# Folding the last two experts' rows into the token sums on TensorE, in a 64-expert kernel on Trainium2

## The reference, cut to what matters

```python
gp = softmax(xt @ w_grp + b_grp); g_p, g_idx = top_k(gp, 1)       # one of 8 groups
e_p, e_loc = top_k(softmax(el_sel), 2); e_p = e_p / sum(e_p)      # two of its 8 experts
weights = g_p * e_p                                               # per token and choice
for each expert e, on the tokens that chose it:
    y = (silu(x @ w1[e]) * (x @ w3[e])) @ w2[e]
h = h + g2 * sum over the two choices of weight * y
out = rmsnorm(h, final_g)
```

## Time and profile before

| | us |
|---|---|
| runs | 2423.55, 2425.97, 2429.41 |
| median of the runs | 2425.97 |
| span of the profiled execution | 2425.2 |
| first expert matmul of the profiled execution | 1452.7 |
| end of the last expert matmul | 2397.4 |
| start of the last DVE operation (L2903) | 2420.84 |

### The profile page before, as it was taken

The page is one execution under the profiler, slowest core; times in us unless marked ns, Lnnn a source line. Parts: engine busy times, 40 slices in busy tenths (PEclk is TensorE's granted clock), DMA queues, the critical chain, the costliest instruction groups (busy, mean ns, idle before and its releaser), DMA issues. The chain is left out here.

```text
span 2425.2 us, 26229 instructions
## 1 busy us (share of the span) xinstructions
PE 2267.0 (93%) x10596; PEld 1416.4 (58%) x10596; DVE 1048.8 (43%) x1730; ACT 718.5 (30%) x1163; POOL 783.4 (32%) x491
## 2 busy tenths in 40 slices
PE   8999999999999999999999999888888888888887
PEld 6676578888887787777777873222222222322233
DVE  6666654443456999746765233111111111211112
ACT  5435643222233333557674221000000000000001
POOL 3335655545553443433336521111111011101000
PEclk9999999999999999999999999999999999999999
DMA  4222243534545243253345269999999999999996
GB/s 161 99 101 68 96 140 113 200 134 162 190 122 139 71 104 109 75 170 120 131 153 205 104 269 412 425 422 424 424 425 425 426 426 425 427 425 426 427 426 272
DMA packets 175417, 598.76 MB, mean 247 GB/s; under 512 B 18098, under 2 KB 96946, under 8 KB 149696
## 3 DMA queue, kind: packets, MB, share of 16 engines
q1 hardware_dynamic: 156000, 564.39, 59.8%
q10 hardware_dynamic: 8704, 24.22, 2.6%
q0 software_dynamic: 10592, 8.46, 1.1%
HBM read 593.19 MB, written 28.97 MB: 257 GB/s over the span
## 5 line engine op out<-in xcount | busy, mean ns | idle before, releaser
L2923 POOL TENSOR_TENSOR ring_r<-ring,ring_r 128x1024 fp32r<-128x1024 f32 (+2 forms) x215 | 513.3, 2393 | 650.2 <-ACT ring_r L1544 650.0
L857 PE MATMUL ps<-r,ring_r 128*128 128x512 f32 x1512 | 605.3, 400 | 3.8 <-POOL ring_r L2923 1.5
L859 PE MATMUL ps<-r,ring_r 128*128 128x512 f32 x1512 | 590.5, 391 | 0.0
L858 PE MATMUL ps<-r,ring_r 128*128 128x512 f32 x1512 | 590.1, 390 | 0.0
L1555 ACT ACTIVATE arena<-ps 128x512 f32<-128x512 f32 (+4 forms) x200 | 150.5, 761 | 1046.8 <-PE ps L1420 852.8
L1420 PE MATMUL ps<-arena 128*64 128x512 f32 x672 | 317.9, 629 | 68.7 <-DMA arena<-in_w 68.5
L1418 PE MATMUL ps<-arena 128*64 128x512 f32 x672 | 328.8, 639 | 0.9 <-DMA arena<-in_w 0.9
L1544 ACT ACTIVATE ring_r<-ring 128x1024 fp32r<-128x1024 f32 x220 | 222.8, 1015 | 351.9 <-PE ps L859 192.1
L857 PEld LDWEIGHTS ps<-r,ring_r 128*128 128x128 f32 x1512 | 282.9, 187 | 75.3 <-issue 10.5
L3028 POOL DMA_INDIRECT y_d<-arena,cbm x64 | 63.7, 995 | 805.0 <-DVE arena L2876 539.6
L858 PEld LDWEIGHTS ps<-r,ring_r 128*128 128x128 f32 x1512 | 282.9, 187 | 64.3 <-issue 5.8
(11 more groups left out here) (377 smaller groups left out, 2550.8 us busy)
## 6 DMA issues: line engine op xcount, KB each, us to landing
arena<-in_w SPq DMA_DIRECT2D x105, 2048.0 KB, 33.7
ring<-in_w SPq DMA_DIRECT2D x86, 2048.0 KB, 37.0
ring<-in_w_ada SPq DMA_DIRECT2D x12, 2048.0 KB, 7.9
ring<-in_ffn_w_in SPq DMA_DIRECT2D x22, 1024.0 KB, 7.6
ring<-in_w_in SPq DMA_DIRECT2D x40, 512.0 KB, 6.2
ring<-in_w_in SPq DMA_DIRECT2D x8, 2048.0 KB, 9.3
ring<-in_fox_w_in SPq DMA_DIRECT2D x7, 2048.0 KB, 8.4
arena<-acs_d SPq DMA_DIRECT2D x16, 512.0 KB, 3.6
```

The costliest lines, as they stand in the source:

```text
L857: e.matmul(out, wh[:, k, :], X.hi[:, k0 + k, :], start=first and k == 0, stop=False)
L858: e.matmul(out, wh[:, k, :], X.lo[:, k0 + k, :], start=False, stop=False)
L859: m = e.matmul(out, wl[:, k, :], X.hi[:, k0 + k, :], start=False, stop=last and k == nk - 1)
L2923: e.tensor_tensor(GL[t], grans[t][1], GH[t].bitcast(F32), ALU.subtract).then_inc(sem["gr_lo"], 1)
```

## The change

Experts 62 and 63 (`LATE`) no longer go through `y_d`. For each of them a matrix of 128 by 512 numbers (`GIVEN`) is made at the start of the expert stage: its row is a seat (the 64 seats stand twice, in partitions 0 to 63 and in 64 to 127), its column a token, its entry the token's weight for that expert if the token sits there, and 0 otherwise. DVE makes it token by seat (`shares`: two operations of 128x4, two of 128x4x64 and one of 128x512 for an expert), PE transposes it (four 128x128 each, use "late"), DVE copies it out of PSUM (`keep_shares`) into places of the constants and parameters that nothing reads any more. ACT's silu of expert 0 waits for `shares`, since it writes over SEAT; ACT's loads of g2 and final_g wait for the transposes.

At the end PE's `late(tt)` multiplies GIVEN with `YO` of 62 and of 63 (for each tile, expert and half one matmul of 64 rows by 128 columns, 512 wide; half 0 in rows 0 to 63, half 1 in rows 64 to 127, each half into its own bank) in the place of `kept(tt)`. The residual is now added by DVE: `second(tt)` makes y1 * weight + h2t, and `total(tt)` adds that to the sums. The rows of `y_d` are read back when the scatters of experts 60 and 61 have landed. Rows that no expert writes any more must be 0, so ACT fills `y_d` with zeros early (4 MiB, DRAM to DRAM, 2048 rows of 2 KB from one row of zeros). The read-back buffers Y and OUT move up by 4096, off the slot of w2[63]. `over_blocks` now stands between the rest of expert 61 and turn(63), and its count is read at n = 32. The last banks are numbered anew.

```diff
+LATE = (NE - 2, NE - 1)
 # bank_table
+        if n == 1:
+            for ex in LATE:
+                t("late", ex)
-            t("my", n - 2)
+            t("my", n - 2, bank=7 if n - 2 == NE - 1 else None)
-            t("sum", tt, half, bank=(4 + 2 * tt + half) % 8)
+            t("sum", tt, half, bank=2 * tt + half)
 # pe
-            for n in range(NE + 2):
+            for n in range(NE):
...
                     turn(n - 1)
+                if n == 1:
+                    for i, ex in enumerate(LATE):
+                        u = ps("late", ex)
+                        w.wait_ge(sem["wk"], 4 + i)
+                        w.wait_ge(u.free, u.n)
+                        for tt in range(4):
+                            m = e.transpose(u.ap[:, 128 * tt:128 * tt + 128], PAIRED[i][:, tt].rearrange("p h x -> p (h x)"), ident)
+                        m.then_inc(u.full, 1)
...
-            over_blocks(e, over_count(e), block)
+            over_blocks(e, over, block)
+            turn(NE - 1)
+            result(NE - 2)
+            result(NE - 1)
...
-                    e.matmul(u.ap, ident, h2t[:, tt, 512 * half:512 * half + 512], start=True, stop=False)
+            def late(tt):
+                for ex in LATE:
+                    uy = ps("my", ex)
+                    w.wait_ge(uy.free, uy.n + 1)
+                    for half in range(2):
+                        u = ps("sum", tt, half)
+                        w.wait_ge(u.free, u.n)
+                        at = slice(64 * half, 64 * half + 64)
+                        e.matmul(u.ap, GIVEN[ex][at, 128 * tt:128 * tt + 128], YO[ex % 2][at, :], start=ex == LATE[0], stop=False)
...
-            kept(0)
-            kept(1)
-            w.wait_ge(osem["end"], 1)
-            kept(2)
-            kept(3)
+            for tt in range(4):
+                late(tt)
             for tt in range(4):
                 gated(tt)
 # act
+            e.dma_start(a["y_d"], a["zeros"].broadcast_to([4 * T, D // 2])).then_inc(sem["out"], 16)
...
+                if ex == 0:
+                    w.wait_ge(sem["wk"], 5)
...
+                    u = ps("late", LATE[1])
+                    w.wait_ge(u.full, u.n + 1)
...
-            over_blocks(e, over_count(e), block)
+            over_blocks(e, over, block)
+            gate_half(NE - 1)
 # dve
+            def shares(j):
+
+                ex = LATE[j]
+                for i in range(2):
+                    e.tensor_tensor(CHOSEN[:, i], OH[i][:, :, ex:ex + 1], WK[i], ALU.mult).then_inc(d.next(), 1)
+                last()
+                for i, dst in enumerate((msel, OHS)):
+                    e.tensor_tensor(dst, SEAT[:, i], CHOSEN[:, i].broadcast_to([128, 4, 64]), ALU.mult).then_inc(d.next(), 1)
+                last()
+                both = [x.rearrange("p t (o x) -> p t o x", o=1).broadcast_to([128, 4, 2, 64]) for x in (msel, OHS)]
+                e.tensor_tensor(PAIRED[j], both[0], both[1], ALU.add).then_inc(sem["wk"], 1)
...
+            def second(tt):
+                y1 = Y[tt][1]
+                w.wait_ge(sem[f"in{tt}"], 16 + 16 + 32)
+                e.scalar_tensor_tensor(y1, y1, KEEP[:, 4 + tt:5 + tt], h2t[:, tt, :], ALU.mult, ALU.add).then_inc(d.next(), 1)
...
-                w.wait_ge(sem[f"in{tt}"], 16 + 16 + 32)
...
-                e.scalar_tensor_tensor(cols(y0, 2), cols(y1, 2), KEEP[:, 4 + tt:5 + tt], PS[:, b:b + 2, :], ALU.mult, ALU.add).then_inc(sem["fc_d"], 1)
+                last()
+                e.tensor_tensor(cols(y0, 2), cols(y1, 2), PS[:, b:b + 2, :], ALU.add).then_inc(sem["fc_d"], 1)
...
+            second(0)
             total(0)
             for tt in range(1, 4):
+                second(tt)
                 total(tt)
                 normed(tt - 1)
             normed(3)
 # sp
-            for ex in (NE - 2, NE - 1):
+            for ex in (NE - 4, NE - 3):
                 u = ps("my", ex)
                 w.wait_ge(u.free, u.n + 1)
-                w.wait_ge(sem[f"yo{ex % 2}"], 16 * NE // 2)
+                w.wait_ge(sem[f"yo{ex % 2}"], 16 * (ex // 2 + 1))
```

More of the change, by code:

```diff
@@ L686, in build_program @@
         SL = [view(10752 + 256 * i, 4, 64) for i in range(2)]
-        EW = [A[:, 12288 + WC * i:12288 + WC * (i + 1)] for i in range(3)]
+        EW = [A[:, 16384 + WC * i:16384 + WC * (i + 1)] for i in range(3)]
         OXG, OXT = XG[0][0:BLK, :], view(2048, 8, BLK)
@@ L1462, in pe @@
                     result(n - 2)
+                if n == 32:
+                    over = over_count(e)
             def block(at, done):
@@ L2028, in gate_half @@
                 e.activation(SL[ex % 2], cols(u.ap, 4)[:, :, 0:64], ACT.Silu).then_inc(sem["sl"], 1)
-            for n in range(NE + 1):
+            for n in range(NE):
+                if n == 32:
+                    over = over_count(e)
                 if n == 2:
+                    u = ps("late", LATE[1])
+                    w.wait_ge(u.full, u.n + 1)
                     for i in range(2):
@@ new lines, in keep_shares, with halved, scaled @@
+            def keep_shares(j):
+                u = ps("late", LATE[j])
+                w.wait_ge(u.full, u.n + 1)
+                e.tensor_copy(GIVEN[LATE[j]], u.ap).then_inc(u.free, 1)
+            def halved(ex):
+                u = ps("mt", ex)
+                w.wait_ge(sem["sl"], ex + 1)
+                e.tensor_tensor(HT[ex % 2], SL[ex % 2], cols(u.ap, 4)[:, :, 64:128], ALU.mult).then_inc(u.free, 1)
+            def scaled(ex):
+                u = ps("my", ex)
+                if ex >= 2:
+                    w.wait_ge(sem[f"yo{ex % 2}"], 16 * (ex // 2))
+                w.wait_ge(sem["g2b"], 32)
+                w.wait_ge(u.full, u.n + 1)
+                e.tensor_tensor(YO[ex % 2], u.ap, G2, ALU.mult).then_inc(u.free, 1)
@@ new lines, in dve @@
+            for n in range(NE):
+                if n % 2 == 0 and n + 2 < NE:
+                    rows(n // 2 + 1)
+                if n == 1:
+                    shares(0)
+                    shares(1)
+                if n >= 1:
+                    halved(n - 1)
+                if n == 1:
+                    keep_shares(0)
+                    keep_shares(1)
+                if n >= 2:
+                    scaled(n - 2)
+                if n == 32:
+                    over = over_count(e)
@@ L3047, in pool @@
             rows(1)
-            for n in range(NE + 2):
+            for n in range(NE):
                 if n % 2 == 0 and n + 4 < NE:
                     rows(n // 2 + 2)
+                if n == 2:
+                    w.wait_ge(sem["out"], 16)
+                if n == 32:
+                    over = over_count(e)
                 if n == 3:
@@ L3184, in sp @@
                 e.dma_start(a["out"][tt * 128:(tt + 1) * 128, :], OUT[tt]).then_inc(sem["out"], 16)
-            w.wait_ge(sem["out"], 64)
+            w.wait_ge(sem["out"], 80)
         block = ctx.enter_context(nc.Block())
@@ L3267, in arrays @@
         "w_mix_out": x["w_mix_out_2"][0], "w1": x["w1_2"][0], "w3": x["w3_2"][0], "w2": x["w2_2"][0],
-        "final_g": x["final_g_2"].reshape(1, D),
+        "final_g": x["final_g_2"].reshape(1, D), "zeros": np.zeros((1, D // 2), np.float32),
     }
```

43 lines of the change are left out of this document (15 added, 28 removed).

## The result

The changed kernel takes **2442.15 us** in the median (2441.13 to 2442.47); in the same comparison the kernel before takes 2427.31 (2423.55 to 2429.41). The ratio is 1.0066, with a 95% interval of 1.0054 to 1.0078: slower, by 14.8 us. The forecast was 2425.0 us, in a range of 2421.5 to 2431.5, so the time lies 10.7 us above the range. The profiled execution has a span of 2440.5 us, against 2425.2.

What follows compares the result with a forecast made beforehand. Weights filling the DMA engines set 2365 us, then 32 us of PE and 28 us of tail; the last operation 0.9 us earlier gave 2425.2 - 0.9 = 2424.3 us profiled, 2425.0 us as median; range 2421.5 to 2431.5 us.

Steps and rivals of the forecast that it cites:

- The zeros: ACT's 4 MiB DMA near 198 us: cost taken as 0; upper bound the transfer's length, 10 to 20 us, little exposed.
- The last of the prediction's signs of being wrong: Last in the list of observations that would prove the forecast wrong: the attention stage is longer; no size given.
- Rival (b): Early stage: zeros hold up ACT or a load, or 2.1 us at 1470 us leave a weight-stream hole; +2 to +6 us, chance 0.12.
- The read-back: Tail: reading y_d waits for expert 61's scatter, so is issued at 2394.4 to 2394.9 us instead of 2402.0, 7.1 us earlier.
- the quiet microsecond: 2394 to 2395 us, DMA engines moving 12 GB/s: taken to show expert 61's scatter lands no later than 2394.2 us.
- PE's late matmuls: Tail: 32 instructions on the chain, halves at once, 0.86 us a pair, from 2397.3 to 2404.3 us.
- rival (a): PE's late matmuls at the end: the halves run one after the other, 1.71 us a pair; +5.8 us, 2431.8 us, chance 0.12.
- DVE's end: Tail: DVE sets the pace, 3.91 us between later totals; last operation starts at 2419.9 us against 2420.84, 0.9 us earlier.
- The start of the expert stage: Near 1466 to 1470 us: shares take 4.0 us, expert 2 is 2.1 us late, full DMA queue covers it; cost 0.
- Where the weights end: End of the expert stage: last wait for a matrix at 2365 us, with 32 us of PE behind it.
- (c): Tail: the rows alone set the end; -7.1 us, 2418.9 us, chance 0.05.
- (d): Tail: nothing moves, as expert 61's scatter lands late or SP's issue is held up; +1.8 us, 2427.8 us, chance 0.06.

## Why the prediction was wrong, point by point

**The zeros: the step that failed.** The prediction took 0 for them, on the DMA share of 0.00 from 200 to 205 us and on ACT's wait for PE, with 10 to 20 us as the transfer's length and "little of it exposed". Each of these failed.
- *The length.* It was worked out from a rate of 200 to 400 GB/s that no row showed for this kind of copy; 40.3 us were measured (4.19 MB, 104 GB/s), two to four times the estimate. No row of the kernel before could have given it, since it has no copy from DRAM to DRAM. The `c_d` reads are no such row, though their 512 KB in 5.1 us, times eight, make 41 us. That is luck: two of them together moved 233 GB/s from 214 to 218 us, and the 5.1 us have about 1 us ahead of the first bytes and the other read's bytes in them.
- *What is due behind it.* I looked 5 us of DMA idleness ahead, and at ACT. With 40 us the question is who reads between 197 and 237 us. In the changed kernel these are four `c_d` reads, two from 213.0 and two from 227.3 us, with POOL and PE directly behind them: POOL waited 18.2 us and PE stood 15.20 us. Even with my own upper bound of 20 us the transfer would have reached to 217 us, over the first `c_d` read at 213.
- *The exposure.* In its order of work PE had nothing else at that place, so the wait came through whole, 15.20 us, and more behind it. These are PE's rows, of the kernel before and then of the changed one:

```profile
226.48 0.60 PE L1077 MATMUL ps<-consts_sb,arena 128*128 128x128 f32 x4
...
229.33 0.82 PE L1077 MATMUL ps<-consts_sb,scr 128*128 128x128 f32 x6
```
```profile
241.82 1.12 PE L1087 MATMUL ps<-consts_sb,arena 128*128 128x128 f32 x4 [15.20 <-POOL arena L3044]
...
244.87 0.63 PE L1055 MATMUL ps<-r,ring_r 128*128 128x512 f32 x1
...
246.78 0.81 PE L1087 MATMUL ps<-consts_sb,scr 128*128 128x128 f32 x6
```

The same work from the first row to the last took 2.85 us and now 4.96, since the granted clock was 0.50 there (0.63 us for a matmul that took 0.39). So PE was 15.3 us late at the end of its wait and 17.4 us late 5 us on, and stayed so to the end of the attention stage. At the gather it is 16.0; the 1.4 us between were won in later stages, to which the change adds nothing. They vary from one execution to the next: by PE's rows the other kernels take from 3.5 us less to 0.6 us more there than the kernel before, in their one profiled execution each.

The 14.8 us of the medians are this term, less the tail's gain. The last of the prediction's signs of being wrong, a longer attention stage, is the one that came. Rival (b) named the mechanism ("the zeros hold up ACT or a load") but gave it +2 to +6 us and a chance of 0.12. The exposed wait was 15.2 us: with that price the rival's time would have been 2425.0 + 15.2 = 2440.2 us, outside the range.

A page of the Trainium skill (DMA: Bandwidth & Descriptors, Queues, rings and completion order) says that a DMA engine takes packets in turn from the queues that have work for it. The trace agrees in part. Of the two `c_d` reads issued from 213.0 us on SP's queue one landed after 19.0 us, ahead of the end of ACT's transfer, the other after 23.7, with it. But in the first ten microseconds, from 213 to 223 us, all 587 packets of data were ACT's and none was SP's (571 and none with the zeros alone in the kernel before); the two queues' packets mix from 223 us on. And the engines were not full meanwhile: from 216 to 223 us their share is 0.37, at 128 GB/s. What held SP's packets back is not shown. Being on another queue gave no shelter from a transfer in front.

**The read-back**: right, and loose by 0.8 us. It was to be issued 2.5 us ahead of E, and was at 1.7:

```profile
2407.60 0.98 POOL L3099 DMA_INDIRECT y_d<-arena,cbm  x1 [3.20 <-DVE arena L2921]
```
```profile
2411.90 2.11 SPq L2101 DMA_DIRECT2D arena<-y_d  x4
```

Expert 61's scatter took 3.6 us to landing and not the 2.32 of the last one. It took 3.6 us in the kernel before as well; the prediction had put the last one's time in its place, and its bound of 2394.2 us, from the quiet microsecond, was 0.8 us too early. The rows were still early enough: DVE waited for the first tile's until 2416.86 us, long before total(0).

**PE's late matmuls**: right. 32 instructions in 7.14 us (7.06 predicted), the halves at once; rival (a), 14 us, is out. Timeline of PE in the changed kernel:

```profile
2415.44 1.03 PE L1518 MATMUL ps<-arena,consts_sb 64*128 64x512 f32 x4
2416.30 1.02 PE L1518 MATMUL ps<-arena,params_sb 64*128 64x512 f32 x4
```

A pair starts 0.86 us behind the other, whichever of the two experts' matrices is loaded.

**DVE's end**: right. total(0) at E + 9.15 (9.1 predicted), from one total to the next 2.55, 3.95 and 3.94 us (2.52, 3.91 and 3.91), from the last total to the last operation 2.96 (3.02), so E + 22.55 against E + 22.5. Two deviations inside it cancel:

```profile
2423.91 1.28 DVE L2957 SCALAR_TENSOR_TENSOR arena<-arena,cbm 128x1024 f32<-128x1024 f32 x1
2425.32 1.22 DVE L2966 TENSOR_TENSOR arena<-arena,ps 128x1024 f32<-128x1024 f32 x1
2426.46 0.16 DVE L2970 RECIPROCAL cbm<-cbm 128x1 f32<-128x1 f32 x1
```

From second to total, which waits for it, it is 1.41 us and not 1.32, and behind the two-operand sum the next operation starts after 1.14 and not 1.20. The Trainium skill's statement (VectorE: DVE Perf Modes, The DRAIN you can't avoid) that a semaphore between chained operations costs nothing extra does not hold in these rows: the dependent operation comes 0.21 us later than an independent one behind the same form (1.20 us, 2426.65 to 2427.85).

**The start of the expert stage**: right, cost about 0. Timeline of DVE's last share and of PE behind it, in the kernel with the zeros in pieces:

```profile
1470.94 0.69 DVE L2903 TENSOR_TENSOR arena<-arena 128x512 f32<-128x512 f32 x1
```
```profile
1471.69 0.66 PE L1475 MATMUL ps<-consts_sb,arena 128*128 128x128 f32 x4 [0.37 <-DVE arena L2903]
```

The shares took 3.4 us (1468.21 to 1471.63; 4.0 predicted), PE waited 0.37 us, and the stage from gather to E is 949.79 us there and 949.97 before. In the changed kernel it is 950.16.

**Where the weights end**: by the prediction's own sign, wrong, at no cost. It put the last wait for a matrix at 2365 us with 32 us of PE behind it. In the changed kernel PE waits for a later matrix:

```profile
2391.33 0.64 PE L1430 MATMUL ps<-arena 128*64 128x512 f32 x1 [1.36 <-DMA arena<-in_w]
```

Less the 16.0 us of delay that is 2375.3 us, with 22.3 us of PE behind it, and so it is in the kernel with the zeros in pieces (2375.62). Before, PE passed this place at 2375.12 us without a wait, 0.2 us sooner, which is the 0.2 us of the result. So the weights still end the stage at the same time, but the sum of 2365 and 32 us does not describe it any more; why the waits moved is open.

**(c) and (d)**: the rows did not set the end, and the tail did get shorter. The sum by the prediction's own terms, with the zeros at what they cost, is 2425.2 + 16.0 + 0.2 - 0.85 = 2440.5 us, the span of the profiled execution. All other terms of the sum were within 0.2 us; the term that was put at nothing was 19 times the gain (16.0 to 0.85).

## What to carry to other kernels

A DMA that fills or broadcasts is priced from a row with the same kind of source, destination and packets, and where there is none its length is measured first. Its whole length is laid against the transfers that are due within it, on every queue, not against the idle engines at its issue. A fill from DRAM wants a source of more than one short row (16 rows of 2 KB were enough here, and made its packets large as well), or a place with nothing due behind it. What a stall costs is more than the stall, if PE's clock is lower behind it (2.1 us on 15.2 here). And where one engine is relieved at the end of a relay, the next one's pace per tile says at once how much of the gain can arrive.

## What the runs showed of the hardware

- Copies from DRAM to DRAM with one row of 2 KB as their source: 10.7 us for 1 MiB, 40.3 and 41.6 us for 4 MiB, 5.7 to 6.2 us for 512 KB. With 2048 source rows 4 MiB took 15.0 us, with 16 rows 15.5 us. The bytes are the same in the three; the source's addresses and the packets (2048 of 2 KB, 64 of 64 KB, 128 of 32 KB) are not, and which of the two decides is open.
- The busy share of the DMA engines says little of the bytes: with the one row 0.96 at 123 GB/s in the changed kernel and 0.71 at 118 in the kernel before with the zeros alone (200 to 215 us in both), with many rows 1.33 at 477 GB/s (195 to 200 us).
- A transfer of 40 us on one queue lengthened reads on another from at most 5.8 to up to 23.7 us, and thereby PE's wait; ones of 15.0 and 15.5 us that ended before they began left them at 5.8 and 6.1 at most.
- PE worked until 226.6 us at a granted clock of 1.00 (2.4 GHz) and then stood until 241.8. From 232 to 237 us the granted clock was 0.50 (1.2 GHz), from 242 to 246 us, with PE at work again, still 0.50, and from 248 to 252 us 1.00. It cost 2.1 us behind the wait (4.96 us for work of 2.85).
